# The operand tiles of x1 and of the mix laid out anew: high and low parts in turns, at multiples of 64 bytes

## The reference, cut to what matters

```
x1 = x + concat(A, M, B) @ w_out                       # the mix, 2048 x 2048
up = causal_dwconv3(rmsnorm(x1) @ w_up)                # 2048 x 12288
y  = x1 + (gelu(gate) * val) @ w_down                  # 6144 x 2048
```

## Time and profile before

| what | value |
|---|---|
| three runs, median | 2290.98 us |
| the profiled execution, its own time | 2290.06 us |
| its span, first to last instruction | 2288.3 us |
| TensorE clock granted | 1.00 throughout |
| PE / PEld busy | 2277.7 us / 2259.1 us, 17856 instructions each |
| DVE / ACT / POOL busy | 1854.8 / 1187.0 / 287.5 us |
| large matmuls (128x272 on forms): b, t, fh | 4176, 5280, 4032 |

### The profile page before, as it was taken

One profiled execution on the slowest core, in us unless ns is written; L12 is line 12 of the kernel. 1 busy time (PEld: TensorE's weight loads), 2 busy tenths in 40 slices (PEclk: granted clock), 3 DMA queues, 4 the chain that ended last, 5 costly groups with the idle time before them and its releaser, 6 DMA issues.

```text
span 2288.3 us, 44911 instructions
## 1 busy us (share of the span) xinstructions
PE 2277.7 (100%) x17856; PEld 2259.1 (99%) x17856; DVE 1854.8 (81%) x2478; ACT 1187.0 (52%) x1911; POOL 287.5 (13%) x241
## 2 busy tenths in 40 slices
PE   9999999999999999999999999999999999999999
PEld 8999999999999999999999999999999999999999
DVE  6788667666888988888888888888888988787876
ACT  4566454444554555455555545555555555454643
POOL 4100000000011011121111111211211110000000
PEclk9999999999999999999999999999999999999999
DMA  9522422323345443444343343433445678686864
GB/s 292 156 76 73 125 85 83 112 80 90 113 145 175 114 122 118 119 128 128 110 136 119 117 138 110 139 117 119 136 120 152 169 199 205 162 209 160 218 145 102
DMA packets 479605, 309.87 MB, mean 135 GB/s; under 512 B 11176, under 2 KB 457640, under 8 KB 479416
## 3 DMA queue, kind: packets, MB, share of 16 engines
q1 hardware_dynamic: 470984, 289.97, 43.1%
q0 software_dynamic: 8432, 17.27, 4.5%
HBM read 255.79 MB, written 53.51 MB: 135 GB/s over the span
## 4 chain that ended last, share of the span: by engine, by line
PE 62%; DVE 2%; issue 1%; ACT 0%; DVEq 0%; ACTq 0%
PE out L2944 21%; PE out L2945 21%; PE out L2946 21%; DVE ring_l L2301 1%; DVE fl L2549 0%; ACT ring_h L1566 0%; DVE pair L2333 0%; DVE s_buf L2313 0%; DVE out L2404 0%; DVE pair L2340 0%; DVE pair L2323 0%; DVE ub L2532 0%; ACT fh L1743 0%; DVE ub L2360 0%; DVE stage L2357 0%
## 5 line engine op out<-in xcount | busy, mean ns | idle before, releaser
L2301 DVE TENSOR_TENSOR ring_l<-pair,ring_h 128x1024 fp32r<-128x1024 f32 (+1 forms) x384 | 455.0, 1185 | 176.2 <-ACT ring_h L1566 176.0
L1566 ACT CAST ring_h<-pair 128x1024 fp32r<-128x1024 f32 (+1 forms) x384 | 383.1, 998 | 323.0 <-DVE pair L2333 227.3
L2944 PE MATMUL out<-t,ring_h 128*128 128x272 f32 x1760 | 507.9, 289 | 2.3 <-DVE ring_l L2301 2.3
L2946 PE MATMUL out<-t,ring_l 128*128 128x272 f32 x1760 | 507.3, 288 | 0.0
L2945 PE MATMUL out<-t,ring_h 128*128 128x272 f32 x1760 | 505.1, 287 | 0.0
L2944 PE MATMUL out<-b,ring_h 128*128 128x272 f32 x1392 | 401.1, 288 | 0.7 <-issue 0.5
L2945 PE MATMUL out<-b,ring_h 128*128 128x272 f32 x1392 | 400.3, 288 | 0.0
L2946 PE MATMUL out<-b,ring_l 128*128 128x272 f32 x1392 | 400.1, 287 | 0.0
L2944 PE MATMUL out<-fh,ring_h 128*128 128x272 f32 x1344 | 387.2, 288 | 2.6 <-DVE ring_l L2301 1.6
L2945 PE MATMUL out<-fl,ring_h 128*128 128x272 f32 x1344 | 386.5, 288 | 0.0
L2946 PE MATMUL out<-fh,ring_l 128*128 128x272 f32 x1344 | 384.2, 286 | 0.0
(11 more groups left out here) (294 smaller groups left out, 3940.9 us busy)
## 6 DMA issues: line engine op xcount, KB each, us to landing
pair<-in_w_up SPq DMA_DIRECT2D x192, 512.0 KB, 4.0
raw<-in_w_in SPq DMA_DIRECT2D x36, 1024.0 KB, 5.7
pair<-in_w_down SPq DMA_DIRECT2D x64, 384.0 KB, 4.7
pair_d<-in_w_down SPq DMA_DIRECT2D x64, 384.0 KB, 4.7
h_forms<-fb SPq DMA_DIRECT2D x24, 816.0 KB, 6.2
fr<-h_forms SPq DMA_DIRECT2D x24, 816.0 KB, 7.4
out_yT<-stage POOLq DMA_DIRECT2D x31, 544.0 KB, 7.9
pair<-in_w_out SPq DMA_DIRECT2D x28, 512.0 KB, 5.0
```

The lines of the kernel that those rows point to most:

```text
L1566: nc.scalar.copy(ring_h[:, n % 3, 0:width(i)], weight_of(p, i)).then_inc(op_hi, 1)
L2301: v.tensor_tensor(ring_l[:, n % 3, 0:w], weight_of(p, i), ring_h[:, n % 3, 0:w].bitcast(F32), ALU.subtract).then_inc(op_lo, 1)
L2944: mm(out, w_high, high[:, k, :], start=opens and k == 0, stop=False, skip_group_check=True)
L2946: ins = mm(out, w_low, high[:, k, :], start=False, stop=k == tiles - 1, skip_group_check=True)
```

## The change

Each form becomes one tensor of 8 tiles x (high, low) x 272: the high tile k and the low tile k stand side by side, 1088 bytes apart, and the next k follows 2176 bytes on. A form with both parts takes 17408 bytes from a multiple of 256, without an offset of its own. The lists of offsets go. X_ROOM goes from 320 to 128, so what lies behind xl moves down by 192 bytes. What is computed, the instructions and their order stay as they are; only the addresses differ, and the writes and reads of a form's 8 tiles step by 2176 bytes and no longer by 1088.

```diff
-B_FIRST = (16, 80, 80, 112, 112, 272)
-T_FIRST = (-112, -16, 48, 112, 112, 112, 128, 320)
-X_ROOM = 320
+X_ROOM = 128
...
         def form_at(name, first):
 
-            lead = first % 32 // 4
-            t = over(name, [P, lead + K8 * HALF], first - 4 * lead, F32R)
-            return t[:, lead:].rearrange("p (k n) -> p k n", k=K8)
-        assert overlay + 6 * form + B_FIRST[-1] <= nc.sbuf_top, nc.sbuf_top - overlay
-
-
-        b_forms = [form_at(f"b{n}", overlay + n * form + B_FIRST[n]) for n in range(6)]
+            t = over(name, [P, K8, 2, HALF], first, F32R)
+            return t[:, :, 0, :], t[:, :, 1, :]
+        assert overlay + 6 * form <= nc.sbuf_top, nc.sbuf_top - overlay
+
+        v22, v21, v11 = (form_at(f"b{n}", overlay + 2 * n * form) for n in range(3))
         sum1 = rstd[:].rearrange("p c n -> p (c n)")
         sq1 = over("sq1", [P, ROWS], wl_at + 16 * K8 * P - 4 * ROWS)
-        x_forms = [form_at(f"t{n}", x_at + n * form + T_FIRST[n]) for n in range(8)]
-        assert T_FIRST[-1] <= X_ROOM and x_at + T_FIRST[0] >= rows_at + 4 * KT * ROWS
-        assert form + T_FIRST[1] + form <= 4 * K8 * ROWS
-
-        v22, v21, v11 = (b_forms[n:n + 2] for n in (0, 2, 4))
-        x_1, x_2, x_3, x_4 = (x_forms[n:n + 2] for n in (0, 2, 4, 6))
+        x_1, x_2, x_3, x_4 = (form_at(f"t{n}", x_at + 2 * n * form) for n in range(4))
+        assert 2 * form <= 4 * K8 * ROWS
...
-        assert slot_at[4] >= overlay + 4 * form + B_FIRST[4]
+        assert slot_at[4] >= overlay + 4 * form
```

## The result

The changed kernel takes 2295.4 us in the median of 15 runs (2294.28 to 2297.74), the kernel before 2290.98 (15 runs on the same chip, 2289.21 to 2292.88): 1.0020 times as long, 95% interval 1.0013 to 1.0027. It is slower by 4.4 us, where the prediction had 5.2 us less, and lies outside the range given. The profiled execution took 2295.03 us.

The account below looks back on a forecast made before the run. PE was taken as the bound, number of matmuls times the cost of one. The terms summed to -5.2 us from the profiled 2290.06 us, 2284.9; with 0.9 to the median, the forecast was 2285.8 us, range 2281.5 to 2292.5.

Parts of the forecast that it names:

- The sign I had called the sharpest: w_up: cells 2 to 46 take 922.2 us in place of 926.05, all seven blocks of a cell alike at 2.994 us.
- (b): Writing the forms on ScalarE and VectorE with 2176-byte steps: at most 1.3 us, taken as 0; casts near 2.01, subtractions 2.42.
- (d): w_up with faster PE: VectorE stays behind PE; 0.2 us of gain eaten at the start, left out.
- a block over 3.01 us: Sign against the prediction: a w_up block of 24 matmuls costing more than 3.01 us.
- (c): X_ROOM moves raw, rings, weights and parameters down 192 bytes: taken as 0 for w_down and w_in.
- My bound of 3.2 us: Largest loss allowed in w_down from the weights' move: 4032 matmuls rising to 125.24 ns.
- 13.44 and 10.52 us: Times of w_down's six blocks and w_in's 84 matmuls, said to stay; if they moved, (c) was wrong.
- (a): Products on forms in w_up and w_out, 9456 matmuls: a mean level of 124.76 ns would save 5.2 us.
- The rival "slower": Forms in w_up and w_out: a dear high-low transition paid by every matmul, 126.25 ns, +8.9 us, 2299.9 us; chance 0.12.
- its 375.9: Cost in ns of three matmuls on forms above which the rival "slower" was to be decided.

Follow-up runs that it names:

- il_320: The changed kernel with X_ROOM = 320 in place of 128, so weights lie as before the change: median 2285.79 us, six runs of 2284.7 to 2288.1, three of 2300.7 to 2302.4.
- il_320_again: The same program as il_320 (changed kernel, X_ROOM = 320), run again: median 2288.15 us, six runs of 2285.3 to 2288.4, two of 2298.9 and 2300.3.
- after_w64: The changed kernel with 192 bytes of room between raw and wh, weights back at 64: median 2299.78 us, four runs of 2286.2 to 2289.0, eight of 2298.7 to 2301.7.
- swap_one: The changed kernel with X_ROOM = 320 and one form of seven, v22, turned round, low tile first: median 2287.85 us, 0.9984 of the kernel before.
- old_w128: The kernel before with 64 bytes of room between raw and wh, weights at 128 modulo 256: median 2296.25 us, 1.0022 of the kernel before.

## Why the prediction was wrong

The steps that held: PE alone sets the time, and the cost of a matmul depends on where operands lie. The sign I had called the sharpest came out: all seven blocks of a cell take the same time. (b) held: casts of 2176 elements take 2010 ns, subtractions 2416. (d) held: no new stops. The prediction had also named as a sign against it a block over 3.01 us, and the blocks take 24 x 125.56 ns = 3.013.

The step that failed is (c), "Taken: 0": X_ROOM, which I had treated as housekeeping. Moving wh, wl and the rings by 64 modulo 256 costs 1.2 us before w_out. w_down went up by 0.37 ns x 4032, 1.5 us less what PE's stops take up, in this pair of traces; since four of seven traces with weights at 64 have the higher level too, how much of that the weights' place costs on average is open. My bound of 3.2 us held w_down's part; for w_in I had a bound for a gain alone. I named 13.44 and 10.52 us as the numbers that would refute it; the first is now 13.48 and the second 10.54.

But (c) also emptied (a). I read the three levels of (a) as properties of the moving tile and its neighbour, while each was a property of moving tile and weight tile together, and all were read with weights at 64. I never asked for the forms themselves what the weights' move would do, so nothing of (c) went into the 9456 matmuls where it counts most. With weights at 128 the new layout runs at 125.56 ns, where I had taken 124.76. The term was 8064 x (124.76 - 125.28) = -4.2 us and measured 8064 x (125.56 - 125.28) = +2.3.

With weights at 64 the new layout does run at 124.8 ns, but 124.76 was luck: it is the mean of three levels of other layouts, and I had no reason for any of them. And it would have carried the forecast only in part. In 13 of the 29 runs of il_320, il_320_again and after_w64 w_up ran at the dear level instead, some 15 us longer, and none of their ratios is clear of 1 on the faster side. Leaving X_ROOM alone would have given the 5 us forecast in some runs and a loss of 10 in others.

The rival "slower" had the right sign and the right point of decision: 3 x 125.56 = 376.7 ns a triple, over its 375.9. Its mechanism, a step from high to low that is dear by itself and that every matmul pays, is refuted: the same steps cost 124.8 with other weights. Its general idea, that alike blocks take the averaging away, is what il_320 shows in another form. The old layout, with seven different blocks, had no long run in 114 (the 15 beside the changed kernel and 99 beside the experiments, none over 2294.5 us); the new one at weights 64 keeps a level for over 900 us once it has fallen into it.

The Trainium skill, "TensorE: Matmul & The Clock Gate", section "Wait — 56ns, not 53.3ns?", gives one distance for all matmuls of a size, which would have meant no change. The runs disagree: 124.4 to 126.7 ns for one instruction at one granted clock.

What stays open is the mechanism itself. The runs show that the cost depends on both operands' places, modulo 256 at least, and on what went before; that the weight load and the moving stream meet somewhere is argued from that, and not shown. I have no rule that gives the level for a new pair of places.

## What to carry to other kernels

When an edit shifts a buffer's start, list every operand behind it, the weights too, and treat a level read from the trace as valid only for the places that it was read with. Where PE is the bound and nothing waits, divide the distance of far-apart starts by the matmuls between them: differences of 0.3 ns in 125 show there and are worth microseconds. Before an even layout is trusted, run it often enough to see whether its times fall into two groups; one block of another pattern per cell was enough here to keep the dear one away in the eleven runs taken.

## What the runs showed of the hardware

The same program, with the same operands' places, runs long stretches of float32r matmuls of 128 x 272 at 124.8 or at 126.67 ns each, both at a granted clock of 1.00; the level changes at a stop of PE, or with no stop (818.75 us in after_w64, 817.64 in swap_one), and a block with high and low in the other order ended it. Weights that start 64, 128 (or 0), 192 and 96 bytes beyond a multiple of 256 gave w_down 124.4 or 124.8, 124.8, 125.6 and 125.9 ns with its moving tiles unmoved modulo 256. After a stop of PE of some 2 us the granted clock was half for some 15 matmuls in one run of il_320 and stayed at 1.00 in another of the same program; in old_w128 it cost about 1.5 us.
